# Attention steps taken in pairs of heads, cross scores in four banks, smaller first loads, the last unit by token tile, and waits placed at the unit that needs them

## What is computed

```python
# first layer
h = rms_norm(x, g_mix) @ w_in            # latents, rotary keys, diff q/k/v
x += concat(mla(8 heads, softmax(q k^T * s) v),
            rms_norm(diff(4 heads, (softmax(q1 k1^T) - lam*softmax(q2 k2^T)) v), g_diff_sub) * 0.8) @ w_out
x += cross(4 heads; q from rms_norm(x, g_xattn), k and v from rms_norm(mem, g_mem)) @ w_xo
x += (silu(hf @ w_gate) * (hf @ w_up)) @ w_down      # hf = rms_norm(x, g_ffn)
x = rms_norm(x, g_final)
# second layer
z = rms_norm(x, g_mix_2) @ w_in_2
x += concat(moba(8 heads; with 256 tokens one block, so plain causal softmax attention),
            silu(rg) * rms_norm(retention(8 heads; (q k^T * decay) v)) * g_ret_2) @ w_o_2
x += (silu(h2 @ w_gate_2) * (h2 @ w_up_2)) @ w_down_2
x += (p_2 @ w_ple_proj_2) * sigmoid(rms_norm(x, g_ple_2) @ w_ple_gate_2 + b_ple_gate_2)
```

## Time and profile before

| | |
|---|---|
| median of 3 runs | 2470.44 us |
| the profiled execution | 2469.99 us, span 2468.2 us |
| PE busy | 2434.5 us |
| PEld, DVE, ACT busy | 2029.3, 1398.0, 1146.3 us |
| `w_hi` on ACT (L746) | 844 times, 1061 ns mean |
| `w_lo` on DVE (L1122) | 844 times, 1225 ns mean |
| PE's share of the chain that ended last | 97% |

### The profile page before, as it was taken

The page is one execution under the profiler, slowest core; times in us unless marked ns, Lnnn a source line. Parts: engine busy times, 40 slices in busy tenths (PEclk is TensorE's granted clock), DMA queues, the critical chain, the costliest instruction groups (busy, mean ns, idle before and its releaser), DMA issues.

```text
span 2468.2 us, 31637 instructions
## 1 busy us (share of the span) xinstructions
PE 2434.5 (99%) x11240; PEld 2029.3 (82%) x11240; DVE 1398.0 (57%) x1554; ACT 1146.3 (46%) x1537; POOL 10.4 (0%) x23
## 2 busy tenths in 40 slices
PE   8999899999999999999999999999999999999998
PEld 6988788888888888888888888888888888888887
DVE  7766555655555555555666655555554555555565
ACT  6555454644434443445554445454443444344453
POOL 0000000000000000000000000000000000000000
PEclk9999999999999999999999999999999999999999
DMA  8645445465555655555555564555555655555554
GB/s 305 214 162 179 144 154 185 148 200 189 190 193 183 196 187 195 195 180 188 171 196 190 177 209 154 191 186 193 179 196 196 189 193 186 193 193 188 180 187 153
DMA packets 125833, 461.97 MB, mean 187 GB/s; under 512 B 13968, under 2 KB 14096, under 8 KB 124960
## 3 DMA queue, kind: packets, MB, share of 16 engines
q1 hardware_dynamic: 123200, 446.75, 55.1%
q0 software_dynamic: 2384, 13.68, 1.6%
q10 hardware_dynamic: 144, 0.07, 0.0%
...
## 4 chain that ended last, share of the span: by engine, by line
PE 97%; DVE 2%; ACT 1%; DMA 1%; issue 0%; ACTq 0%; SPq 0%; DVEq 0%
PE acc L422 90%; PE pt L478 2%; PE acc L427 2%; PE acc L572 1%; PE po L618 1%; DVE w_lo L1122 1%; PE po L610 0%; PE pt L589 0%; DMA raw<-stream 0%; ACT w_hi L746 0%; DMA vec<-vectors 0%; PE acc L556 0%; ACT mix_hi L765 0%; DVE mix_lo L1226 0%; DVE mix_lo L1219 0%
## 5 line engine op out<-in xcount | busy, mean ns | idle before, releaser
L1122 DVE TENSOR_TENSOR w_lo<-raw,w_hi 128x1024 fp32r<-128x1024 f32 x844 | 1029.5, 1225 | 943.3 <-ACT w_hi L746 936.2
L746 ACT ACTIVATE w_hi<-raw 128x1024 fp32r<-128x1024 f32 x844 | 894.2, 1061 | 1234.8 <-PE acc L422 1191.4
L422 PE MATMUL acc<-w_hi,norm_hi 128*128 128x512 f32 (+1 forms) x2240 | 881.2, 394 | 0.0
L422 PE MATMUL acc<-w_hi,norm_lo 128*128 128x512 f32 (+1 forms) x2240 | 869.5, 388 | 0.0
L422 PE MATMUL acc<-w_lo,norm_hi 128*128 128x512 f32 (+1 forms) x2240 | 596.2, 388 | 0.0
L422 PEld LDWEIGHTS acc<-w_lo,norm_hi 128*128 128x128 f32 x2240 | 419.4, 188 | 86.6
L422 PEld LDWEIGHTS acc<-w_hi,norm_lo 128*128 128x128 f32 x2240 | 420.8, 188 | 84.1
L422 PEld LDWEIGHTS acc<-w_hi,norm_hi 128*128 128x128 f32 x2240 | 420.7, 188 | 83.9
L422 PE MATMUL acc<-w_hi,mix_hi 128*128 128x512 f32 x1088 | 428.6, 394 | 9.3 <-DVE mix_lo L1414 4.5
L422 PE MATMUL acc<-w_hi,mix_lo 128*128 128x512 f32 x1088 | 425.5, 391 | 0.0
L422 PE MATMUL acc<-w_lo,mix_hi 128*128 128x512 f32 x1088 | 292.0, 390 | 0.0
...
## 6 DMA issues: line engine op xcount, KB each, us to landing
raw<-stream SPq DMA_DIRECT2D x844, 512.0 KB, 3.3
...
```

Of the source, the lines that this page charges most:

```text
L422: last = pe.matmul(acc[:, slot, c * NB:c * NB + width], a[:, k * T + c * P:k * T + (c + 1) * P], w[:, s, kk * width:(kk + 1) * width], sta ...
L746: act.activation(w_hi[:, (units.fixed - 1) % RING, :], src, ACT.Copy).then_inc(w_hi_ready, 1)
L1122: dve.tensor_tensor(w_lo[:, s, :], src, w_hi[:, s, :].bitcast(F32), ALU.subtract)\
```

## The change

- MLA and MoBA heads are stepped in pairs: both scores at slot 3, both transposes at 6, both values at slot 3 of the next block; ACT and DVE likewise (`exps_of`, `copies_of`, `keep_of`, `maxima_of`, `normalise_of`, `split_heads`), with both `normalise` at slot 5.
- Diff heads move within their two blocks; `turn_diff(0)` goes from slot 6 to 7, `diff_scale(0)` behind `normalise(11)`, `kept_low(8)` into slot 0 of the residual block. That block's first need is relaxed: its first units ask only for the operands they multiply by.
- Retention heads go in pairs, four per block; `ret_scale` is cut into `ret_norm` and `ret_gate`, and the last block holds only `turn_ret(0)`.
- Cross attention: all four heads' scores first, in four banks, then transposes and values; ACT copies half of the queries (`queries_ready`).
- `hidden_low` in the MLP stands one subtraction earlier.
- The first loads: the memory tokens come in parts of 2, 2, 4, 4 and 4 of their 16 chunks between the first units, and POOL's loads wait for the second part; the head gains are loaded later.
- The last unit of the last block is multiplied one token tile after the other, and the gate's steps and the store go by tile as well.

The diff, cut to its core (a line such as @@ PE @@ marks whose program follows):

```diff
 SCORED.update({N_MOBA + h: B_AQ + 6 + h // 2 for h in range(A_H)})
-SCORED.update({N_RET + h: B_AQ + 11 + h // 3 for h in range(R_H)})
+SCORED.update({N_RET + h: B_AQ + 11 + h // 4 for h in range(R_H)})
 def slot_of(n):
-    return SCORED[n] % 2 if n in SCORED else n % 2
+    return SCORED[n] % 2 if n in SCORED else (B_XQ - JOBS[n][1] // 2) % 2
 def scores_of(n):
-            at = 0 if kind in ("diff", "cross") else n % 2 * 2 * T
+            at = 0 if kind == "diff" else n % 2 * 2 * T
 def probs_of(n):
-                return (tmp_a, tmp_b, tmp_d)[n % 3]
+                return (tmp_a, tmp_b)[h // 2][:, h % 2 * 2 * T:(h % 2 + 1) * 2 * T]
+        def stat_of(t, n):
+            return t[:, h // 2, h % 2 * TT:(h % 2 + 1) * TT] if kind == "cross" else t[:, n % 3, :]
...
+        MEM_PARTS = ((0, 2), (2, 4), (4, 8), (8, 12), (12, 16))
@@ SP @@
-            for b in range(NBD):
-                load_mem(b)
-                if b < RING // 2:
-                    load(2 * b, 2 * b)
-                    load(2 * b + 1, 2 * b + 1)
+            for i in range(2):
+                load_mem(i)
+                load(i, i)
+            load_mem(2)
+            for r in range(2, RING):
+                load(r, r)
+            load_mem(3)
+            load_mem(4)
...
+            for t in range(TT):
+                sp.wait_ge(out_ready, NBD + t)
+                sp.dma_start(out[:, (t + 1) * D - NB:(t + 1) * D], x[:, (t + 1) * D - NB:(t + 1) * D])\
+                    .then_inc(out_stored, 16)
@@ POOL @@
+            pool.wait_ge(mem_landed[1], 16)
             pool.dma_start(con[:, :], consts).then_inc(con_landed, 16)
             pool.dma_start(pos[:, TT:].bitcast(I32), positions).then_inc(con_landed, 16)
-            pool.dma_start(gain_rows[:, :], head_rows.broadcast_to([P, 2 * P])).then_inc(con_landed, 16)
@@ PE @@
+                    if by_tile and ki == n_units - 1:
+                        pe.wait_ge(raw_read, units.value())
+                        for t in range(TT):
+                            passes(((w_hi, act_hi), (w_hi, act_lo)), False, (t,))
+                            last = passes(((w_lo, act_hi),), False, (t,))
+                            last.then_inc(w_used if t else tile_used, 1)
+                        continue
...
             def attend(n0, n_jobs):
-                for i in range(n_jobs + 3):
-                    if i < n_jobs:
-                        scores(n0 + i)
-                    if 2 <= i < n_jobs + 2:
-                        transposes(n0 + i - 2)
-                    if i >= 3:
-                        values(n0 + i - 3)
+                for i in range(n_jobs):
+                    if i == 2:
+                        pe.wait_ge(queries_ready, 1)
+                    scores(n0 + i)
+                for i in range(n_jobs + 1):
+                    if i < n_jobs:
+                        transposes(n0 + i)
+                    if i:
+                        values(n0 + i - 1)
...
-            whole({0: lambda: transposes(1), 1: lambda: (turn_rotated(), values(1)), 2: lambda: scores(2),
-                   4: lambda: scores(3), 5: lambda: transposes(2), 6: lambda: values(2), 7: lambda: transposes(3)})
+            for n in range(2, MLA_H, 2):
+                whole({1: turn_rotated, 3: lambda: (values(n - 2), values(n - 1), scores(n), scores(n + 1)),
+                       4: turn_keys if n == MLA_H - 2 else lambda: None,
+                       6: lambda: (transposes(n), transposes(n + 1))})
-            whole({0: lambda: values(7), 1: lambda: (turn_rotated(), scores(8)), 4: lambda: scores(9),
-                   5: lambda: transposes(8)})
-            whole({0: lambda: transposes(9), 1: lambda: (values(8), scores(10)), 2: lambda: values(9),
-                   4: lambda: scores(11), 5: lambda: transposes(10), 6: lambda: turn_diff(0)})
+            whole({1: turn_rotated, 2: lambda: (values(6), values(7), scores(8)),
+                   5: lambda: (transposes(8), scores(9))})
+            whole({1: lambda: (transposes(9), values(8), scores(10)), 4: lambda: (transposes(10), values(9), scores(11)),
+                   7: lambda: turn_diff(0)})
...
-                     first_need=lambda ki: (operand_ready, base + (ki * UK >= 12)))
+                     first_need=lambda ki: (operand_ready, base - (ki * UK < 8) + (ki * UK >= 12)))
...
+            for n in range(N_RET, len(JOBS), 4):
+                whole({1: lambda: (scores(n), scores(n + 1)),
+                       3: lambda: (values(n), values(n + 1), scores(n + 2), scores(n + 3)),
+                       5: lambda: (values(n + 2), values(n + 3))})
+            whole({3: lambda: turn_ret(0)})
@@ ACT @@
+            def exps_of(n):
+                exps(n)
+                exps(n + 1)
...
-            during(NU, {0: lambda: keep(3), 1: lambda: evicted(DQ + CB), 2: lambda: column_root(r_mem), 3: lambda: exps(4),
-                        5: lambda: (exps(5), copy_transposed(4)), 6: lambda: keep(4), 7: lambda: copy_transposed(5)})
+            during(NU, {1: lambda: evicted(DQ + CB), 2: lambda: column_root(r_mem), 3: lambda: keep_of(2),
+                        4: lambda: exps_of(4), 6: lambda: copies_of(4)})
...
-                        4: lambda: column_root(r_head[:, 0, 0:4]), 5: lambda: (exps(11), copy_transposed(10)),
-                        6: lambda: kept_hi(8, "g_diff_sub", (0, 1, 0, 1))})
+                        4: lambda: (copy_transposed(10), keep(9)),
+                        5: lambda: (exps(11), column_root(r_head[:, 0, 0:4])),
+                        7: lambda: kept_hi(8, "g_diff_sub", (0, 1, 0, 1))})
...
-            split(NU - 4)
+            split(NU - 5)
             load_table(ACT.Exp)
+            act.wait_ge(w_used, units.value(RING - 1))
+            act.activation(chunks(heads, XQ + 2, 2), acc[:, taken.fixed % 2, 2 * T:], ACT.Copy)\
+                .then_inc(queries_ready, 1)
             taken.add()
+            split(1)
@@ DVE @@
                     for b in range(NBD):
-                        split(3)
+                        split(2)
                         if b == 0:
                             hidden_low(n - 1)
-                        elif last:
+                        split(1)
+                        if b and last:
                             turned_low(b - 1, next_name)
...
+            def maxima_of(n):
+                maxima(n)
+                maxima(n + 1)
+            def normalise_of(n):
+                normalise(n)
+                normalise(n + 1)
...
-            during(NU, {0: lambda: split_head(3), 1: mem_mean, 2: lambda: maxima(4), 3: lambda: normalise(4),
-                        4: lambda: maxima(5), 5: lambda: normalise(5), 6: lambda: (split_head(4), rotate_wide()),
-                        7: scale_keys})
+            during(NU, {1: mem_mean, 3: lambda: (maxima_of(4), split_heads(2)), 5: lambda: normalise_of(4),
+                        6: rotate_wide, 7: scale_keys})
...
-            during(NU, {1: lambda: maxima(10), 3: lambda: (head_mean(2 * P, EPS_DIFF, DIFF_H // 2, 0, 4), normalise(10)),
-                        4: lambda: maxima(11), 5: lambda: diff_scale(0),
-                        6: lambda: (normalise(11), take_token_major(NU, DV, 8 * P, 1, r_col)),
-                        7: lambda: kept_low(8, "g_diff_sub", (0, 1, 0, 1))})
+            during(NU, {1: lambda: maxima(10), 3: lambda: normalise(10), 4: lambda: maxima(11),
+                        5: lambda: head_mean(2 * P, EPS_DIFF, DIFF_H // 2, 0, 4),
+                        6: lambda: (normalise(11), diff_scale(0), take_token_major(NU, DV, 8 * P, 1, r_col))})
-            residual(NU, "g_xattn", {2: lambda: (head_mean(2 * P, EPS_DIFF, DIFF_H, 1, 4), diff_scale(1)),
+            residual(NU, "g_xattn", {0: lambda: kept_low(8, "g_diff_sub", (0, 1, 0, 1)),
+                                     1: lambda: head_mean(2 * P, EPS_DIFF, DIFF_H, 1, 4), 2: lambda: diff_scale(1),
                                      3: lambda: kept_low(12, "g_diff_sub", (0, 1, 0, 1))})
...
-            took(dve.tensor_copy(chunks(heads, XQ), block_end(NU)))
+            took(dve.tensor_copy(chunks(heads, XQ, 2), block_end(NU)[:, 0:2 * T]))
...
-            during(NU, {0: lambda: ret_scale(0), 1: lambda: maxima(n + 6), 3: lambda: maxima(n + 7),
-                        5: lambda: kept_low(8, "g_ret_2", range(4)),
-                        6: lambda: (head_mean(P, EPS, DIFF_H + R_H, 1), gate(chunks(heads, RG + CB))),
-                        7: lambda: column_inverse(r_head[:, 1, :])})
+            during(NU, {0: lambda: (ret_gate(0), ret_norm(1)), 4: lambda: kept_low(8, "g_ret_2", range(4)),
+                        6: lambda: (gate(chunks(heads, RG + CB)), ret_gate(1))})
...
+            b = NBD - 1
+            split(NU)
+            dve.wait_ge(tile_used, 1)
+            biased(acc[:, taken.fixed % 2, :], b, 0).then_inc(tile_taken, 1)
+            took(biased(block_end(NU), b, 1))
+            for t in range(TT):
```

(4 more changed lines are left out.)

240 lines of the change are left out of this document (125 added, 115 removed).

## The result

The kernel after takes 2481.19 us (median of 5, 2481.13 to 2482.56) against 2470.44 before: slower by 0.45%, ratio 1.0045 with a 95% interval of 1.003 to 1.006. The forecast was 2481. One execution of the experiment `best`, of six, took 3055.03 us at a mean granted clock of 0.753 against 0.999 or more in the other five, and is left out of the comparisons.

What follows compares the result with a forecast made beforehand. PE is busy 99% of the span, so time is its matmuls plus its waits. Added 29.45 less gone 18.65 gives +10.8 on 2469.99, 2480.8; the median 0.45 above makes the forecast 2481 us, range 2473 to 2488.

Steps and rivals of the forecast that it cites:

- the clockwork of one unit: Weight ring: DVE's job of a slot starts 2.34 us after its unit ends; units last 2.73, leaving 0.4 of room.
- MLA and MoBA pairs: Four blocks each: PE waits for the second head's normalising, longer behind exposed table loads; 6.3 and 4.7 us added.
- a rival of 0.08: More clock falls behind new idle stretches of 1.75 to 2.2 us: up to 11.8 us more, 2493; chance 0.08.
- Diff heads: Diff heads and the residual block behind: new PE waits, plus 2.35 us of half clock twice; 18.45 us added.
- The least visible step: Residual block: `transposes(11)` waits through `turns_read()` for `kept_low(8)`, since both write `pt`; 4.1 us idle, 2.35 more from the clock.
- What goes: Old PE waits at the diff turns, residual block, `turn_ret(1)` and MLP hidden blocks disappear: 14.65 us saved.
- The start: First loads: PE begins about 1.5 us earlier but waits for the fifth weight unit's chain; gain 0.3, between 0 and 1.5.
- Cross attention: Halved query copy gains 0.5 us, ACT's copy delays the subtraction ahead of the first maximum 0.5; nothing, -1 to +1.
- The end: Last unit, gate steps and store by token tile: 1.6 us from half operations, 0.8 from the store; 2.4 saved.
- covered slots: Rival: DVE reaches slot jobs within 0.7 us of the unit's end, one-slot waits vanish; 2460.3 us, faster; chance 0.12.
- the free `pt`: Rival: `kept_low(8)` is done when head 11 is turned, so sharing costs nothing; 2474.8 us, no change; chance 0.13.
- the drain: Rival: each of four exposed table loads also costs a drain of about 1.4 us; 5.5 more, 2486.8; chance 0.05.

Runs made afterwards that it cites:

- best: `both` with `cross_late`, the exponential's table loaded behind the first diff half's root, and head 11's transposes and the second half's steps one slot later: 2450.88 us.
- pairs_t7: The kernel after with the transposes of every MLA and MoBA pair, and ACT's copies of them, at slot 7 instead of 6: 2468.39 us.
- cross_late: The kernel after with DVE's subtraction of one weight unit moved from ahead of cross attention to behind it: 2479.61 us.
- low7: The kernel after with `kept_low(8)` back at slot 7 of its own block, one subtraction earlier than slot 0 of the residual block: 2475.70 us.
- both: The kernel after with pairs transposed at slot 7 and the diff heads spread to leave two slots between normalising and transposing: 2456.48 us.
- tables: The kernel after with ACT's exponential table loaded at slot 2 of the first and third MLA and first MoBA block, ahead of the exponentials: 2476.02 us.

## Why the prediction was right

- What bounds the kernel, and the clockwork of one unit: right. The eight waits at pairs stand where a slot leaves 0.4 us of room for 1.65 of work, and two slots remove them (`pairs_t7`).
- MLA and MoBA pairs, 6.3 and 4.7: measured 2 x 1.03 + 2 x 2.47 = 7.0, and 3 x 0.96 + 2.2 = 5.1. The part missed is the loss of overlap when PE stops, about 0.16 at each stop; beyond it, clock drops behind the long ones, 1.3 and 1.6 in the profile. In the prediction they were a rival of 0.08. They came at none or two of the three long waits in each profile: a term of 0 to 3 us, not a case of its own.
- Diff heads, 18.45: waits 3.4 + 4.8 + 4.3 + 1.3 = 13.8 against 13.75 forecast. The half clock came out smaller in this profile: 1.7 each lost in the windows 309 to 313 and 320 to 323, against 2.35. The slow stretch was half as long as that of the earlier trace rows, which lasted from 301 to 308. That is chance and not the kernel: in the profile of `cross_late`, the same program up to there, the first of the two lasts from 307.5 to 314.3, and in that of `pairs_t7` the same two waits of 4.8 and 4.3 are followed by stretches from 300.7 to 307.6 and from 311.0 to 317.8, which cost 2.3 each after PE had resumed, the price of the prediction. A row of a stretch at half clock, in the kernel after:

```profile
320.00:321.00 1.00, 1.00 (x4) 0.82 (x3) 0.00 (x0) 0.60 (x1) 0.00 (x0) 0.50 0.38 152
```

- The least visible step, `transposes(11)` through `turns_read()`: right in place and size (4.1, measured 4.3), and proved by `low7`.
- What goes: right. The waits of the first MLP, of retention and of the second MLP vanish (-1.2, -1.3, -1.3 with the switches in them), and so does the 4.5 at the residual block. The front matter laid `hidden_low` on L1226; the row names L1219, the subtraction of the helper `low`, which `hidden_low` and `split_head` both call.
- The start, 0.3 out of 0 to 1.5: wrong. It gained 1.8 in this profile, outside my own bounds, and nothing in the profiles where the clock fell behind the seventh unit's wait. That PE would wait there was foreseen, the drop of the clock was not; PE's first weight unit began at 6.74, where I had said 8.4. I held the transfer of the earlier trace rows to be fixed by the bytes ahead of it; it was issued 3 us earlier because its place in the ring came free earlier, and POOL's loads no longer ran beside it.
- Cross attention, 0 within -1 to +1: right. The +0.8 of the profile is the drop of the clock there: without one the stretch takes 31.15 (`low7`) and 31.13 (`both`) against 31.27 before. The mechanism that I had named, ACT's copy delaying a subtraction ahead of the first maximum, costs 0.8 (`cross_late`) where I had said 0.5, and the rest of the change makes up for that.
- The end, 2.4: 2.57 in the profile, 2.85 alone.

The errors ran against each other. In the profile the start was 1.5 better than forecast and the half clock at the diff heads 1.3 cheaper; pairs cost 1.1 more, and drops of the clock in MLA, MoBA and cross attention, for which the sum had nothing, cost 1.3 + 1.6 + 0.9 = 3.8. Together that is +2.1 against the 1.8 between 12.6 and 10.8; small terms make up the rest. The median execution stands at +10.75, presumably with fewer drops (not shown). That the forecast met the median to 0.2 us is partly luck; that it was slower by waits of one slot, and which, is not. Of the rivals, covered slots and the free `pt` are refuted by the waits themselves, the drain by `tables`.
